# One weight stream for both token groups: the second group's input projection is folded into the first group's

## What is computed

```python
h = rmsnorm(x, norm_g)
z = h @ w_in                         # q, k, v, r, a_low, gu, gv, xq, gates: 2048 -> 15376 columns
q, k, v, r, a_low, gu, gv, xq, gates = split_columns(z)
branch_a = rmsnorm(gla_chunked(q, k, v, log_a, s0)) * silu(r)      # gated linear attention, chunks in order
branch_b = gmlp_spatial_gate(gelu(gu), gelu(gv), ...)
branch_c = memory_attention(xq, mem_k, mem_v)
merged = sum over b of sigmoid(gates_b) * (branch_b @ w_br_b)
x = x + merged @ w_out
# PEER: product keys choose 8 x 16 = 128 experts for each token, out of 16384
a = einsum(u_tab[idx], h2)           # one 2048-wide row of peer_u per (token, expert)
x = x + einsum(gate * gelu(a), v_tab[idx])   # one row of peer_v per (token, expert)
y = rmsnorm(x)
```

## Time and profile before

| what | value |
|---|---|
| median of 3 runs | 5190.8 us (5189.43 to 5200.47) |
| the profiled execution | 5193.47 us, its span 5191.7 us, granted TensorE clock 0.876 |
| PE busy | 4025.0 us (78%) |
| DVE busy | 3155.2 us (61%) |
| ACT busy | 835.6 us (16%) |
| moved by DMA | 1592.84 MB, mean 307 GB/s |
| chain that ended last | PE 54%, DMA 20%, DVE 12% |

### The profile page before, as it was taken

The page is one execution under the profiler, slowest core; times in us unless marked ns, Lnnn a source line. Parts: engine busy times, 40 slices in busy tenths (PEclk is TensorE's granted clock), DMA queues, the critical chain, the costliest instruction groups (busy, mean ns, idle before and its releaser), DMA issues.

```text
span 5191.7 us, 59325 instructions
## 1 busy us (share of the span) xinstructions
PE 4025.0 (78%) x22704; PEld 3607.9 (69%) x22704; DVE 3155.2 (61%) x4031; ACT 835.6 (16%) x1046; POOL 1384.2 (27%) x824
## 2 busy tenths in 40 slices
PE   6998999879898999999967889899999996411000
PEld 6998999768787877788755667778888886311000
DVE  5333333443454577626647767779786713799998
ACT  3334443422233200001011000000000000000000
POOL 0000000000000133304311323343333512377887
PEclk9999889879899999999978989999999998655555
DMA  4555775526453799979964989999989978799999
GB/s 168 202 200 189 262 264 200 173 99 228 140 202 130 299 423 423 423 307 368 406 209 174 411 310 399 411 423 422 382 334 383 423 272 320 304 392 388 406 420 383
DMA packets 347714, 1592.84 MB, mean 307 GB/s; under 512 B 36994, under 2 KB 153266, under 8 KB 172252
## 3 DMA queue, kind: packets, MB, share of 16 engines
q0 software_dynamic: 114288, 830.54, 39.1%
q1 hardware_dynamic: 233236, 759.77, 39.0%
HBM read 1501.96 MB, written 88.22 MB: 306 GB/s over the span
## 4 chain that ended last, share of the span: by engine, by line
PE 54%; DMA 20%; DVE 12%; issue 5%; POOL 3%; DVEq 2%; ACT 2%; SPq 1%; ACTq 0%; POOLq 0%
PE psum L485 19%; PE psum L2410 15%; PE psum L522 11%; DMA sb_raw<-in_wstream 11%; DVE sb_acc_b L2255 6%; POOL sb_ring L2163 3%; DMA sb_gt<-dram_zb 2%; DMA sb_ring<-in_peer_v,sb_idx_all 2%; DMA sb_ring<-in_peer_u,sb_idx_all 2%; DMA sb_raw_u<-in_wstream 1%; DMA sb_oh<-dram_e 1%; PE psum L687 1%; DVE sb_acc L2255 1%; DVE psum L2541 1%; DVE sb_split L469 1%
## 5 line engine op out<-in xcount | busy, mean ns | idle before, releaser
L2163 POOL DMA_INDIRECT sb_ring<-in_peer_v,sb_idx_all x512 | 996.8, 1947 | 1269.4 <-DVE sb_acc L2255 981.1
L485 PE MATMUL psum<-sb_actr,sb_split 128*128 128x264 f32 x8112 | 1043.4, 292 | 49.8 <-DVE sb_split L469 22.8
L485 PEld LDWEIGHTS psum<-sb_actr,sb_split 128*128 128x128 f32 x8112 | 1033.6, 197 | 54.4 <-issue 51.7
L522 PE MATMUL psum<-sb_hxb,sb_raw 128*128 128x256 f32 x3872 | 857.9, 381 | 50.1 <-DMA sb_raw<-in_wstream 48.1
L469 DVE TENSOR_TENSOR sb_split<-sb_raw,sb_split 128x2048 fp32r<-128x2048 f32 x201 | 460.7, 2293 | 710.1 <-ACT sb_split L465 709.5
L522 PEld LDWEIGHTS psum<-sb_hxb,sb_raw 128*128 128x128 f32 x3872 | 728.7, 190 | 179.1 <-DMA sb_raw<-in_wstream 81.2
L2250 DVE CUSTOM_DVE_ANT_0 sb_ring<-sb_ring,sb_htok 128x2048 f32<-128x2048 f32 x264 | 600.0, 2291 | 253.2 <-DMA sb_ring<-in_peer_u,sb_idx_all 224.3
L2163 POOL DMA_INDIRECT sb_ring<-in_peer_u,sb_idx_all x256 | 341.9, 1336 | 1290.1 <-DVE sb_dots L2250 613.9
L2255 DVE SCALAR_TENSOR_TENSOR sb_acc<-sb_ring,sb_coef,sb_acc 128x2048 f32<-128x2048 f32 x256 | 601.8, 2351 | 103.3 <-DMA sb_ring<-in_peer_v,sb_idx_all 84.4
L2255 DVE SCALAR_TENSOR_TENSOR sb_acc_b<-sb_ring,sb_coef_b,sb_acc_b 128x2048 f32<-128x2048 f32 x256 | 601.8, 2351 | 30.0 <-DMA sb_ring<-in_peer_v,sb_idx_all 2.6
L2410 PE MATMUL psum<-sb_h,sb_raw_u 128*128 128x256 f32 x2752 | 603.3, 381 | 17.3 <-DMA sb_raw_u<-in_wstream 15.2
(11 more groups left out here) (351 smaller groups left out, 3385.5 us busy)
## 6 DMA issues: line engine op xcount, KB each, us to landing
sb_raw<-in_wstream SPq DMA_DIRECT2D x428, 1024.0 KB, 5.9
sb_raw_u<-in_wstream SPq DMA_DIRECT2D x86, 1024.0 KB, 14.9
sb_states<-in_state SPq DMA_DIRECT2D x32, 512.0 KB, 3.4
out_gla_s<-sb_states SPq DMA_DIRECT2D x32, 512.0 KB, 3.2
dram_a<-sb_a_stage SPq DMA_DIRECT2D x128, 128.0 KB, 10.3
sb_oh<-dram_e SPq DMA_DIRECT2D x16, 1024.0 KB, 7.5
dram_za<-sb_zst SPq DMA_DIRECT2D x121, 132.0 KB, 1.8
sb_vrow<-dram_v SPq DMA_DIRECT2D x8, 1024.0 KB, 5.9
```

The costliest lines, as they stand in the source:

```text
L485: last = nc.tensor.matmul(psum[:, 2 * pair, 0:ntok], w[a], acts[:, b, kt, 0:ntok], start=(i == 0 and a == 0 and b == 0), stop=(i == len(kt ...
L522: last = nc.tensor.matmul(bank_b(q), raw[:, (n - N_XQ) % 3, w0 + i * P:w0 + (i + 1) * P], acts[:, kt, 0:WB], start=(i == 0), stop=(i == le ...
L2163: nc.gpsimd.indirect_dma_start(ring[g % RING][:], None, ins[table], bass.IndirectOffsetOnAxis(ap=col, axis=0)) \
```

## The change

The separate stage (`sp_project_b`, `act_project_b`, `pe_project_b`) is gone. The norm and the split of group B's x are made during the memory projection, and in projection A each split weight block is used for both groups: 48 matmuls for A into one PSUM bank, then 48 for B into the next. The results of both go side by side into one DRAM array `z` of 520 columns. DVE's `beside(184)` becomes `beside(1)` and the counts in the later stages are raised. `act_soft` and `act_gelu` move to later places in ACT's order.

```diff
-        PLAIN = [(N_MEM0, N_XQ, ACT.Copy, MEM), (N_XQ, N_LOW, ACT.Copy, WA), (N_LOW, N_GU, ACT.Copy, WA),
+        PLAIN = [(N_MEM0, N_XQ, ACT.Copy, MEM), (N_XQ, N_LOW, ACT.Copy, WZ), (N_LOW, N_GU, ACT.Copy, WZ),
...
 def pe_project(pe):
-                    products(pe, slot, memr if ntok == MEM else actr, range(KT), 0, slot, ntok).then_inc(out_ready, 1)
+                    if ntok == MEM:
+                        last = products(pe, slot, of_mem, range(KT), 0, 2 * slot, MEM)
+                    else:
+                        products(pe, slot, of_a, range(KT), 0, 2 * slot, WA)
+                        if isinstance(n, int) and n == N_XQ:
+                            pe.wait_ge(act_lo, 9)
+                        last = products(pe, slot, of_b, range(KT), 0, 2 * slot + 1, WB)
+                    last.then_inc(out_ready, 1)
...
 def act_project(act):
+                    w = min(ntok, WA)
+                    last = nc.scalar.activation(zst2[:, slot, 0:w], pair_of(slot, w), func, bias=bias)
+                    if ntok == WZ:
+                        last = nc.scalar.activation(zst2[:, slot, WA:WZ], psum[:, 2 * slot + 1, 0:WB], func, bias=bias)
+                    last.then_inc(evac_done, 1)
...
 def dve_norm_x(dve, n):
+            if n in (9, 10):
+                dve.wait_ge(squares_ready, 6)
+                t = slice((n - 9) * CH, (n - 8) * CH)
+                last = nc.vector.tensor_reduce(ssumb[:, t], sqb[:, :, t].rearrange("p k t -> p t k"), AX.X, ALU.add)
...
 def dve_gla(dve, g, beside=lambda k: None):
-            beside(3)
+            beside(5)
...
-            beside(2)
+            beside(3)
...
 def norm(u):
-                beside(1)
+                beside(3)
...
 def dve_out_b(dve, beside):
-            beside(1)
+            beside(6)
...
-            beside(38)
+            beside(42)
...
 def act_table(act):
+                if i == 10:
+                    act_soft(act, 1)
...
+                if i == 50:
+                    act_gelu(act, 2)
                 if i == 78:
+                    act_gelu(act, 3)
                     act_soft(act, 4)
-                if i == 114:
+                if i == 119:
                     act_soft(act, S_T)
...
 def dve_table(dve, beside):
-                beside(2 if i % 3 == 0 else 1, U_ROWS)
+                beside(3 if i % 4 == 0 else 2, U_ROWS)
...
 def _(sp):
             sp_out(sp)
-            sp_project_b(sp)
             sp_gla(sp, GB)
...
 def _(act):
             act_out(act)
-            act_project_b(act)
             act_gla(act, GB)
             act_attention(act, GB)
             act_spatial(act, GB)
+            act_soft(act, 0)
+            act_gelu(act, 0)
+            act_gelu(act, 1)
             act_out_b(act)
...
 def _(dve):
-            beside(184)
+            beside(1)
             dve_gla(dve, GB, beside)
-            dve_merge_b(dve, N_BA, N_BC, beside, 2)
+            dve_merge_b(dve, N_BA, N_BC, beside, (3,))
             dve_attention(dve, GB, beside)
-            dve_merge_b(dve, N_BC, N_BB, beside, 1)
+            dve_merge_b(dve, N_BC, N_BB, beside, (2, 1))
             dve_spatial(dve, GB, beside)
-            dve_merge_b(dve, N_BB, N_OUT, beside, 1)
+            dve_merge_b(dve, N_BB, N_OUT, beside, (2, 1))
             dve.drain().then_inc(merged_ready, 1)
             dve_out_b(dve, beside)
-            assert gone[0] > 330, gone
+            assert 205 < gone[0] < 240, gone
...
 def _(pe):
             pe_out(pe)
-            pe_project_b(pe)
             pe_gla(pe, GB)
```

More of the change, by code:

```diff
@@ L476, in wait_piece, with products @@
                 pe.wait_ge(act_lo, k + kt // 4 + 1)
-        def products(pe, slot, acts, kts, w0, pair, ntok, ready=None):
+        def products(pe, slot, acts, kts, w0, bank, ntok, ready=None):
             for i, kt in enumerate(kts):
@@ L1113, in dve_gla @@
         def dve_gla(dve, g, beside=lambda k: None):
+            if g.samples:
+                for k in range(2):
+                    dve.wait_ge(st_out[k], 16 * TS * HEADS // 2)
             for f in range(8):
@@ L1484, in dve_attention @@
                 if h + 2 < HEADS:
-                    beside(1)
+                    beside(2)
                     maxima(h + 2)
@@ L1581, in dve_merge_b @@
                 for j, (row, _) in enumerate(outputs_of(n)):
-                    beside(rows)
+                    beside(rows[j])
                     q = out_b(n) + j
@@ L1806, in sp_out @@
             wide_loop(sp, N_WQ, N_END - 2, lambda n, slot, u, m, j: load_block(sp, n + 2, slot))
-            for n in range(N_XQ, N_XQ + 3):
+            for n in range(N_BA, N_BA + 3):
                 load_b(sp, n)
@@ L2348, in z_stores_u @@
         def z_stores_u(k):
-            last = max(n for n in range(N_XQ, N_BA) if z_slot(n) == k % 4)
-            return z_use_b(last) + k // 4
+            return Z_A[k % 4] + k // 4
         def sp_table(sp):
```

272 lines of the change are left out of this document (126 added, 146 removed).

## The result

The changed kernel takes 5272.7 us (median of 4 runs, 5266.5 to 5275.7), the kernel before 5190.1 us beside it (5183.8 to 5200.5): a ratio of 1.0156, interval 1.0136 to 1.0175. It is slower by 82.6 us; the forecast was 5254 us, slower by 64. The profiled execution took 5266.5 us, with a span of 5264.8.

What follows compares the result with a forecast made beforehand. PE was taken to bound the projections, DMA at 422 GB/s most row stages, DVE the last rows: 5193.5 - 282 (projections) + 345 (183 moved rows) = 5256.5 us profiled, 5254 as median; range 5165 to 5345.

Steps and rivals of the forecast that it cites:

- The removed stage and the products: Projection B's whole window, 907 us, goes; PE's added products in projection A cost 121 blocks x 5.73 = 693 us.
- The term "-58": Projection A: two thirds of its 86 us of waits for splits and low-clock blocks taken back; bounds nothing and 86.
- The norm of group B: Query projection: moving the norm of group B's x out of it saves 18 us, some 4 us of waits staying.
- GLA B: Seven more rows and one more choice in this DVE, ACT and PE chain: +18 us, bounds 11 and 25.
- Merge B to the queries: 47 more rows in this 620 us stretch: +105 us, between +57 at 422 GB/s and +129 at its own mean.
- The table: 117 more rows in the table: 457 MB, end at 1100 to 1110 us, +195, bounds +150 and +230.
- DVE falls behind, ACT holds PE's banks at these three places: In the table, at blocks 50, 78 and 119, ACT waits for rows: holds of about 50, 58 and 110 us.
- The first: From 2656 to 4496 us idle DMA time takes the rows up: end 5139 us; chance 0.22.
- The second: Table and stretch ahead of it: mixed DMA rate only 397 GB/s, end 5345 us; chance 0.06.
- the third: Table and stretch ahead of it: mixed traffic limited to 348 GB/s, end 5557 us; chance 0.02.
- The fourth: Each moved choice and row stands bare on DVE, rows cost 410 us: 5319, or up to 5386; chance 0.08.
- The fifth: Projection A: the clock falls in 1400 us of dense matmuls; at 0.94, +90 us; chance 0.02.

## Why the prediction was right, and where it was not

**The total.** The forecast of +64 us against +83 measured is better than its parts. The gain was put 51 us too low and the price of the rows 61 us too low, and that these cancel is luck. The signs, and which side wins, were right for the reasons given: the rows cost more in their new places than the fold gives.

**The removed stage and the products.** 907 us forecast and 908 found. Projection A ended near 1604 us, not 1650, and so only 4 us from where the forecast would have called itself wrong: all 86 us of waits went, where I took back 58, and a state update takes 1.70 us from start to start, where the sum had 1.94 (8 us over 32). Without the updates a block is (1450 - 32 x 1.70) / 121 = 11.53 us, 11.55 in the forecast. The term "-58" was mis-sized, at its bound.

**The norm of group B.** -33 in place of -18: the 16 query blocks now take 95 us in one piece, where they and the norm took 119.5. That is 24 of the 33; the other 9 were not traced. The memory projection's +8 came out as +9.

**GLA B.** +34, outside the bounds of 11 to 25. The moved rows without the fold cost 26 us here, just above the bound that knew VectorE's rows only. The rest goes for the most part with the load of `w_up` at the stage's start: PE waits 14.5 us for it, 8.0 before and 8.1 with the rows moved and no fold. In the kernel after, the first six gathers are issued from 2321.4 to 2327.8 us, right beside that load; without the fold they lie in projection B. The run with 8 of these rows emptied gives 24 us back (202 to 178), and its wait for `w_up` is 6.8.

**Merge B to the queries.** +129, at the upper bound. The bounds knew only bytes; VectorE's share was in a sentence, not in a number. It is the two bounds of 667 and 690 us, and 61 us of gaps above the higher one.

**The table.** +211, forecast +195 with bounds of 150 and 230. The size was right, the mechanism half. The bytes are right: 463.96 MB at 413 GB/s on average (forecast 457 MB). But the step "DVE falls behind, ACT holds PE's banks at these three places" does not happen in this kernel: DVE waits 6.4 us for a softmax, ACT never for dots. The forecast took PE to run at 6.91 us a block until a hold; instead the weight loads share the bandwidth with the gathers from the first block on, PE waits 160 us in 78 pieces, and the rows keep their place. The run with the stores on ScalarE's queue shows the holds, 131 and 113 us, and the same total. That the sum of three holds came near what the bytes ask for is luck; had the bytes been fewer, the wrong mechanism would have given a wrong number.

**The last stage.** +32 for +27; the exchange of the samples ends 63 us behind PE's last block, near the 70 forecast.

**The rivals.** The first (idle DMA time takes the rows up, 5139 us) failed where it was put: 2.2 us a row, above the 1.54 of its break-even. The second (397 GB/s) and the third (348) fail by the table's 423. Of these the third is the one for which the Trainium skill speaks (DMA: Bandwidth & Descriptors, Where 436 GB/s comes from), with about 358 GB/s from HBM for a core: the trace after, with one core running, has means of 423 and 421 GB/s over 424 and 600 us of weights and gathers, so this case doesn't bear it out. The fourth (bare ACT and DVE waits, 5319 us and up) is out by the total and, in the table, by the run with VectorE's work gone. The fifth is out: the granted clock is 1.00 over the 1450 us of products.

**What stays open.** Not tried were pacing in the table, and a fold of only some blocks, which would leave enough of projection B for the rows. Why the 20 and 36 rows moved into the table made it longer (two bunches of rows) is argued from PE's waits, from the run with two of five rows emptied and from the pacing in projection B, and not shown by a run of its own. The 53 us of the 11 choices and the 48 emptied rows are not separated.

## What to carry to other kernels

A stage that PE bounds may be the cover of another stream; removing it is worth its length less what that stream costs where it must go, and that price goes up to the bytes over the full rate where the DMA is full (an estimate of 2.49 us a row at 422 GB/s; the table paid 238 us for 115 rows, 2.1 each, since without them it was bound by PE and had some DMA time idle), with gaps on top where VectorE is nearly full as well. Before moving work out of a stage, look whether it is only bunched there: two windows of the stage with different GB/s, with PE waiting for weights in the first, are a sign that a wait which paces the rows may give for one line what a rewrite was meant to give (62 of 71 us here). And a wait that the profile puts down to one engine says who was last, not what was scarce: move one queue and it goes to another engine at the same total.

## What the runs showed of the hardware

- One core's DMA moved 423 GB/s on average over 424 us and 421 over the next 600, with gathers of 128 rows of 8 KB and loads of 1 MB mixed. The last 256 rows, gathers with little else, ran at 398 (397 before), so the mixture was no slower.
- With the DMA full, a store of 128 KB took 35.1 us (median) from issue to landing behind 1 MB loads in the same queue; on a queue of its own ScalarE's wait for it fell from 851 to 410 us in the table, and nothing was gained.
- PE ran its split products for 1450 us with 5 us of gaps, one of 256 or 264 columns each 0.12 us (11.53 / 96), at a granted clock of 1.00; a plain fp32 block of 16 products takes 6.91 us, 0.43 us a product.
